# A two-pass RWKV-7/pooling trunk: the second pass projects r, key, value and low-rank columns for two blocks per product

## The chip, the cores and the metric

The kernel runs on one core of a Trainium2 chip. The metric is the device time of one execution in microseconds. The kernel before takes 2581.55 us (median of 3 runs, 2581.06 to 2581.68).

## What is computed

Sequence length 4096, width 1024, one layer. Cut to what matters here:

```python
u = rms_norm(h, norm_gain) * (1.0 + scale) + shift
proj = u @ w_in                      # 1024 -> 3200 columns
y_pool = multiscale_pool(proj[pool value]) * silu(proj[pool gate])
# RWKV branch: pf = proj columns r | k | v | w_down | a_down
pf = pf + (token_shift(pf) - pf) * mu           # token t needs token t-1
w_log = -softplus(-(w0 + tanh(wd) @ w_lora_up)) - 0.5;  decay = exp(-exp(w_log))
a = sigmoid(a0 + ad @ a_lora_up)
kk = normalized(k * k_k);  k = k * (1 + (a - 1) * k_a)
# per head, a 64x64 state S, in order of time:
#   S = S*decay + (S @ -kk) outer (kk*a) + v outer k;   y = S @ r
y_rwkv = group_norm(y) + bonus(r, k, v);  y_rwkv *= silu(proj[rwkv gate])
h = h + gate * (concat(y_pool, y_rwkv) @ w_out);  out = rms_norm(h, final_gain)
```

All arithmetic is float32.

## The kernel before

The kernel has two passes. The first (`first_pass`, 8 tiles of 512 tokens) does the norm, the pooling branch and its half of the output product, and stores two things in DRAM: the partial result (`h1`) and the normalized input, transposed, as `xt` (32 blocks of 128 tokens, for each block and partition 8 x 128 numbers in one piece). The second pass (`second_pass`) does the RWKV branch in 32 blocks of T2 = 128 tokens, each made of two chunks of 64.

The TensorE program of one block n is `front(n)`, then `back(n)`. `front` has the head variance of block n-1, the bonus sum (`rk_sum`, bank 1), transposes of v and of the key pair BK, and the Gram products of both chunks (line 1348). `back` has six inversion steps (lines 1238 and 1241), and then for both chunks: products with the state (line 1270, called R below), the solve (1281), the state product (1294) and the output products (1302, 1303). VectorE and ScalarE take each result out of PSUM and prepare the next operand. Between two inversion steps, VectorE masks and transposes (`factor`, lines 1774 and 1786), and ScalarE copies the step's result to LX (`take_step`, line 1493); step i+1 waits for both.

While all that happens, TensorE fills its time with the **projection of the next block**: 17 column tiles of 128 weights (13 of r, key, value and low-rank columns, 4 of the gate), each of 8 products over the 1024 inputs. They are cut in **slots** of 4 products, 34 per block, that `fill(k)` puts between the other work: 6 slots before step 0, 3 after each of steps 0 to 3, 2 after step 4, 1 after step 5, then 2, 2, 1 and 2 between the chunk's products, and the rest, 6, at the end of `back`. The first 20 slots of a block use 128 columns of weights per instruction (line 1183), the last 14 use `by_halves`, two products with 64 columns of weights each (line 1164). A float32 product is two MATMUL records in the trace.

The tiles come in five groups of PSUM banks 0 and 1 in turn (`GROUPS`, line 1105):

```python
GROUPS = [(12, 1, 0), (0, 4, 1), (4, 4, 0), (8, 4, 1), (13, 4, 0)]   # first tile, tiles, bank
```

When a group is complete (`group_ps`), ScalarE's `take_group` copies it, scaled by mu, one column to the right (line 1432, `prev`), and VectorE's `shift` (line 1675) adds the token-shift mixture into `mix`. Only then may the bank be used again. The column of the last token is carried to the next block by a copy on GpSimd (line 1617). ScalarE and VectorE run their instructions strictly in the written order: on ScalarE `take_group` 0 stands before `take_step(0)`, group 1 before `take_step(3)`, group 2 before the low-rank exponentials and `take_u(0)`, group 3 after `take_u(1)`, the gate group at the end. On VectorE, the way from the state sum of chunk 1 to the next block's step 0 is one long row of operations: the key (lines 1714, 1715), `shift` 3, BK (1722), the operands LA (1813, 1819), the state, the bonus (1825), masks of the Gram products (1830, 1835), WT and W (1791, 1786).

SyncE loads the transposed input of block n+2 (`load_xT`, line 1129) when the projection of block n is complete. The prologue (line 1384) projects block 0 in one go during the end of the first pass.

Of the kernel before, what the change touches and what calls it, by code (L numbers as in the profile page):

```python
# [126 lines left out]
def build(nc, A, out):  # L127
# [3 lines left out]
    with ctx:  # L131
# [42 lines left out]
        W2 = ((0, 4, 0), (4, 4, 4096), (8, 4, 8192), (13, 4, 12288), (12, 1, 16384))  # L174
# [786 lines left out]
        def second_pass():  # L961
# [10 lines left out]
            xT = [new(f"xT2{j}", [P, KT, T2]) for j in range(2)]  # L972
            mix = new("mix", [P, MIX, T2])
            prev = new("prev", [P, MIX, 1 + T2])
# [4 lines left out]
            egx = new("egx", [P, NP, T2])  # L979
# [3 lines left out]
            t2 = new("t2", [P, NP, T2])  # L983
            k2 = new("k2", [P, NP, T2])
            rk = new("rk", [P, NP, T2])
# [42 lines left out]
            group_ps = signal("group_ps", 5)  # L1028
            rg_ready = signal("rg_ready", 1)
            mix_in = signal("mix_in", MIX)  # L1030
            mix_ready = signal("mix_ready", 4)
            carry_ready = signal("carry_ready", 1)
# [10 lines left out]
            gprev_ready = signal("gprev_ready", 1)  # L1043
            exps_ready = signal("exps_ready", 3)
# [111 lines left out]
            def tensor(pe):  # L1156
# [10 lines left out]
                def project(m, n, par, prologue=False, halves=False):  # L1167

                    gr, q, k0 = SLOTS[m]
                    t0, w, b = GROUPS[gr]  # L1170
                    if q == 0 and k0 == 0:
                        if gr == 0:
                            pe.wait_ge(xT_loaded[par], (n - par) * 8 + 16)
                            if not prologue:
                                s.wait(bt_ready, 2)
                        elif gr > 1:
                            nx.wait(mix_ready, gr - 1)
                        elif not prologue:
                            s.wait(prep_ready, 1)
                        if prologue:  # L1180
                            pe.wait_ge(w2_in[[g[0] for g in W2].index(t0)], 32 if t0 == 12 else 16)
                    for k in range(k0, k0 + KT // 2):
                        last = (by_halves if halves else nc.tensor.matmul)(  # L1183
                            bank[b][:, q * P:(q + 1) * P], w2_tile(k, t0 + q), xT[par][:, k, :],
                            start=(k == 0), stop=(k == KT - 1))
                    if q == w - 1 and k0:
                        last.then_inc(group_ps.sem, 1)

                def low_rank():
                    nx.wait(mix_ready, 1)  # L1190
                    nx.wait(th_ready, 1)
                    for p in range(NP):
                        for i, (part, rhs) in enumerate(((slice(0, LORA), th[0:LORA, :]), (slice(LORA, P), mix[LORA:P, 12, :]))):
# [28 lines left out]
                def inverses(fill, other, first):  # L1222
# [31 lines left out]
                    fill(1, halves=True)  # L1254
# [51 lines left out]
                def front(n, first=False):  # L1306
# [16 lines left out]
                    for p in range(NP):  # L1323
                        for r, c in QUARTERS:
                            j = int(r == c)
                            last = nc.tensor.matmul(bank[(5, 7)[j]][half(c), p * HD:(p + 1) * HD], mix[half(r), 8 + p, j * C:(j + 1) * C],
# [25 lines left out]
                def back(n, first=False, ahead=True, par=0):  # L1352
# [6 lines left out]
                    def fill(k=1, halves=False):  # L1359
                        for _ in range(k):  # L1360
                            if ahead and m[0] < len(SLOTS):
                                project(m[0], n + 1, 1 - par, halves=halves)
# [6 lines left out]
                    if ahead:  # L1369
                        low_rank()  # L1370
                    solve(0)
                    fill(2, halves=True)
                    state_and_output(0, first)
                    fill(2, halves=True)
# [3 lines left out]
                    fill(1, halves=True)  # L1378
                    solve(1)
                    fill(2, halves=True)  # L1380
                    state_and_output(1)
                    fill(len(SLOTS), halves=True)

                def prologue():
                    nx.block(0)
                    pe.wait_ge(sum_ready1.sem, sum_ready1.at(N1 - 1, 7 * PT))
                    for m in range(len(SLOTS)):
                        project(m, 0, 0, prologue=True)
                    low_rank()
                    key_norm()  # L1390

                def blocks():
# [3 lines left out]
                    front(1)  # L1396
                    back(1, par=1)
                    front(2)
                    for n in range(2, N2 - 3, 2):
                        back(n)  # L1400
                        front(n + 1)
                        back(n + 1, par=1)
                        front(n + 2)
                    back(N2 - 2)
                    front(N2 - 1)
                    back(N2 - 1, ahead=False, par=1)
# [7 lines left out]
            def scalar(act):  # L1414
# [5 lines left out]
                def take_group(n, gr):  # L1420
# [3 lines left out]
                    t0, w, b = GROUPS[gr]  # L1424
                    nx.wait(group_ps, gr + 1)
                    if gr == 4:
# [8 lines left out]
                def exp_tanh():  # L1435
                    hd.wait(mix_ready, 1)
# [551 lines left out]
```

## Time and profile before

| | us |
|---|---|
| median of 3 runs | 2581.55 |
| the profiled execution | 2582.14 |
| its span, first to last instruction | 2580.4 |
| PE busy | 2489.7 (96%) |
| PEld (weight loads) busy | 2054.8 (80%) |
| DVE busy | 1657.4 (64%) |
| ACT busy | 1147.4 (44%) |
| POOL busy | 415.3 (16%) |
| mean granted TensorE clock | 0.984 |

The first pass and the prologue end at about 763 us, where the second pass's first inversion step starts; the regular blocks then take about 57 us each, and the last block ends the span. PE is the matrix product on TensorE, PEld its weight loads, DVE is VectorE, ACT ScalarE, POOL GpSimd. A busy PE is not a PE at its peak, since records of products overlap. What a product costs is therefore read from the distance of starts.

### The profile page before, as it was taken

Reading aid. Unit: us, or ns where it says so; the run is one execution under the profiler, and the core shown is the slowest. Engines: PE = TensorE matmul, PEld = TensorE weight load, DVE = VectorE, ACT = ScalarE, POOL = GpSimd, SP = SyncE. Lnnn points to the kernel's source line nnn. Section 1 sums busy time; section 2 is a strip of 40 time slices with the busy share of each in tenths; the row PEclk is TensorE's granted clock in tenths of the full one; section 3 lists DMA queues with packets and bytes.
Section 4 is the critical chain, followed back from the end, with each engine's and each line's share of the span. In section 5 each row is a group of like instructions: output and inputs, shape, how many; then the busy total and the mean of one; then the engine's idle time right before and its main releaser. Section 6 shows DMA issues by size and latency. Waiting matters only on the chain.

```text
span 2580.4 us, 73686 instructions
## 1 busy us (share of the span) xinstructions
PE 2489.7 (96%) x30485; PEld 2054.8 (80%) x30485; DVE 1657.4 (64%) x3459; ACT 1147.4 (44%) x2539; POOL 415.3 (16%) x565
## 2 busy tenths in 40 slices
PE   4999999999999999999999999999999999999995
PEld 4777666777768888888888888888888888888883
DVE  4563344334357777777777777767777777777774
ACT  4332223331124555454455554544555445455552
POOL 1410111110111111111111111211111112111110
PEclk7999999999999999999999999999999999999997
DMA  6613321334510010000001010000110000001000
GB/s 236 208 63 130 130 98 56 114 122 172 187 50 10 35 35 33 28 26 26 26 26 43 26 35 26 26 26 26 35 35 28 33 26 26 26 26 43 26 19 25
DMA packets 72618, 152.91 MB, mean 59 GB/s; under 512 B 3801, under 2 KB 38190, under 8 KB 71342
## 3 DMA queue, kind: packets, MB, share of 16 engines
q1 hardware_dynamic: 68878, 141.62, 15.6%
q10 hardware_dynamic: 3488, 7.34, 0.8%
q8 instruction: 231, 3.78, 0.6%
q14 instruction: 21, 0.17, 0.0%
HBM read 98.61 MB, written 50.33 MB: 58 GB/s over the span
## 4 chain that ended last, share of the span: by engine, by line
PE 85%; DVE 9%; issue 3%; ACT 1%; DMA 1%; SPq 0%; DVEq 0%; ACTq 0%
PE banks L1183 21%; PE banks L383 15%; PE banks L1164 14%; PE banks L1218 9%; PE banks L459 9%; PE banks L1238 7%; DVE SM L1830 2%; PE banks L1281 1%; PE banks L1294 1%; PE banks L1194 1%; PE banks L1348 1%; PE banks L1270 1%; DMA gc<-in_w_ada 1%; PE banks L1302 1%; PE banks L1303 1%
## 5 line engine op out<-in xcount | busy, mean ns | idle before, releaser
L1183 PE MATMUL banks<-xT,wts 128*128 128x128 f32 x5232 | 633.7, 279 | 0.0
L1183 PEld LDWEIGHTS banks<-xT,wts 128*128 128x128 f32 x5232 | 598.2, 192 | 30.9 <-issue 27.1
L1493 ACT ACTIVATE LX<-banks 128x512 f32<-128x512 f32 (+1 forms) x384 | 185.0, 524 | 643.4 <-DVE WT L1774 437.3
L1164 PE MATMUL banks<-xT,wts 128*64 128x128 f32 x6944 | 420.1, 274 | 0.0
L1164 PEld LDWEIGHTS banks<-xT,wts 128*64 128x64 f32 x6944 | 380.2, 137 | 6.3
L1610 POOL TENSOR_TENSOR BK<-k,egi 64x512 f32<-64x512 f32 x64 | 96.0, 1500 | 930.4 <-ACT egi L1462 889.4
L1218 PE MATMUL banks<-wo,Y 128*128 128x512 f32 x512 | 233.8, 600 | 4.7 <-DVE Y L1734 4.7
L383 PE MATMUL banks<-ts,wts 128*128 128x256 f32 x1024 | 233.3, 381 | 0.0
L1774 DVE TENSOR_TENSOR WT<-banks,level_mask 128x256 f32<-128x256 f32 x256 | 102.6, 422 | 194.8 <-PE banks L1238 186.8
L459 PE MATMUL banks<-wo,yc 128*128 128x512 f32 x512 | 224.1, 596 | 0.0
L383 PEld LDWEIGHTS banks<-ts,wts 128*128 128x128 f32 x1024 | 195.9, 191 | 27.5 <-DVE fgain L845 0.5
L459 PEld LDWEIGHTS banks<-wo,yc 128*128 128x128 f32 x512 | 97.0, 192 | 118.6 <-issue 118.5
L383 PE MATMUL banks<-xT,wts 128*128 128x256 f32 x768 | 180.2, 383 | 6.7 <-ACT xT L563 4.7
L1599 POOL TENSOR_TENSOR LA<-SM,ones 64x256 f32<-64x256 f32 x128 | 93.4, 730 | 529.0 <-DVE Y L1734 515.2
L1432 ACT ACTIVATE prev<-banks,vec 128x128 f32<-128x128 f32 x416 | 121.8, 374 | 120.4 <-PE banks L1183 114.0
L1218 PEld LDWEIGHTS banks<-wo,Y 128*128 128x128 f32 x512 | 93.7, 193 | 100.4 <-issue 94.8
L383 PEld LDWEIGHTS banks<-xT,wts 128*128 128x128 f32 x768 | 146.8, 192 | 30.4 <-ACT xT L563 5.4
L1238 PEld LDWEIGHTS banks<-LX,W 64*64 64x64 f32 x4096 | 111.9, 134 | 58.0 <-issue 50.3
L1238 PE MATMUL banks<-LX,W 64*64 64x128 f32 x4096 | 143.1, 278 | 2.5 <-ACT LX L1493 1.6
L1675 DVE SCALAR_TENSOR_TENSOR mix<-banks,omu,prev 128x128 f32<-128x128 f32 x416 | 119.3, 345 | 27.7 <-ACT prev L1432 10.3
L845 DVE TENSOR_TENSOR fgain<-banks,fgain 128x256 f32<-128x256 f32 x96 | 40.7, 424 | 138.0 <-PE banks L383 137.7
L1786 DVE STREAM_TRANSPOSE W<-WT 128x256 f32<-128x256 f32 x320 | 121.8, 419 | 0.0
(193 smaller groups left out, 3649.1 us busy)
## 6 DMA issues: line engine op xcount, KB each, us to landing
wo<-in_x SPq DMA_DIRECT2D x8, 2048.0 KB, 9.4
xt_dram<-xT SPq DMA_DIRECT2D x32, 512.0 KB, 8.6
xr<-in_x SPq DMA_DIRECT2D x32, 512.0 KB, 5.7
h_dram<-xr SPq DMA_DIRECT2D x32, 512.0 KB, 2.7
xT<-xt_dram SPq DMA_DIRECT2D x32, 512.0 KB, 3.3
gate_row<-h_dram SPq DMA_DIRECT2D x32, 512.0 KB, 3.4
out<-gate_row SPq DMA_DIRECT2D x32, 512.0 KB, 2.6
wts<-in_w_in SPq DMA_DIRECT2D x4, 2048.0 KB, 7.9
```

Of the source, the lines that this page charges most:

```text
L383: last = nc.tensor.matmul(product_ps(g, i), w1[:, g, left, k], right[:, k], start=(k == 0), stop=(k == KH - 1))
L459: last = nc.tensor.matmul(bank[BANK_OUT[h]][:, :], yc[:, k, j * P:(j + 1) * P], wo1[:, k, h * 512:(h + 1) * 512], start=(k == 0), stop=(k ...
L1164: last = nc.tensor.matmul(o[half(c)], lhsT[:, half(c)], rhs, start=start, stop=stop)
L1183: last = (by_halves if halves else nc.tensor.matmul)(bank[b][:, q * P:(q + 1) * P], w2_tile(k, t0 + q), xT[par][:, k, :], start=(k == 0), ...
L1218: last = nc.tensor.matmul(bank[(4, 7)[h]][:, :], Y[:, p], wo2[:, p, h * 512:(h + 1) * 512], start=(p == 0), stop=(p == NP - 1))
L1238: last = nc.tensor.matmul(step_banks[a][half(c), j, p * P:(p + 1) * P], W[h, a, j, p], (LX if i else AI)[h, a, j, p].rearrange(flat), star ...
L1432: nx(nc.scalar.activation(prev[:, t, 1:], src, ACT.Copy, scale=v("mu", t)), mix_in, hold=False)
L1493: s(nc.scalar.activation(to, of, ACT.Copy), lx_ready, hold=False)
L1610: hd(nc.gpsimd.tensor_tensor(BK[h, :, :, 1 - e], chunks(k2[h]), chunks(egi[h]), ALU.mult), kt_ready if e else head_pool)
L1675: ins = nc.vector.scalar_tensor_tensor(out=mix[:, t], in0=bank[b][:, q * P:(q + 1) * P], scalar=omu[:, t:t + 1], in1=prev[:, t, 0:T2], op0 ...
L1774: s(nc.vector.tensor_tensor(WT[:, a], left(a)[:, :, 0:2, 0], mask_of(level_mask[i]), ALU.mult), wt_ready, hold=False)
L1786: s(nc.vector.transpose(W[:, a].rearrange("p j q t -> p (j q t)"), WT[:, a].rearrange("p j q t -> p (j q t)")), w_ready, hold=False)
```

## The change

The 13 tiles of r, key, value and low-rank columns are no longer projected for one block at a time, but for two, with 256 columns of x per product. What was one list of groups is now two, in turn. While an even block's back runs, the next, odd, block is projected: tile 12 and tiles 4 to 9 for that block and the one after it. While an odd block's back runs, the next, even, block is projected: tiles 0 to 3, 10 and 11 for that block and the one after it. The gate's 4 tiles stay with one block. All products now have 128 columns of weights; `by_halves` is no longer used in the projection. A slot is 2 products of 256 columns, or 4 of the gate's: 36 slots in the first list, 32 in the second. The positions and numbers of `fill` are unchanged but for the rest at the end.

`mix` holds two blocks; `prev` only holds one group per bank; the last token's column is kept in `carry`, by small copies on ScalarE in `take_group`, and the copy on GpSimd is gone. `egx`, its subtraction on VectorE and its exponential on ScalarE are gone; `decay` has one more column per chunk, set to 1, instead. `xT` holds two blocks side by side for each of the 8 input tiles, so that a load now writes 8 pieces of 512 bytes per partition, where it wrote one of 4096. The order in which w_in's columns lie in `wts` is changed. The prologue projects the first list for block 0 alone and the second list for blocks 0 and 1.

```diff
-            GROUPS = [(12, 1, 0), (0, 4, 1), (4, 4, 0), (8, 4, 1), (13, 4, 0)]
-            MIXED = [1, 5, 9, 13]
-            SLOTS = [(gr, q, k) for gr, (_, n, _) in enumerate(GROUPS) for q in range(n) for k in (0, KT // 2)]
+            GROUPS = ([(0, 2, 0), (2, 2, 1), (10, 1, 0), (11, 1, 1), (13, 4, 0)],
+                      [(12, 1, 0), (4, 2, 1), (6, 2, 0), (8, 2, 1), (13, 4, 0)])
+            GATE = 4
+            SLOTS = [[(gr, q, k) for gr, (_, w, _) in enumerate(g) for q in range(w) for k in range(0, KT, KT // 2 if gr == GATE else KT // 4)]
+                     for g in GROUPS]
...
-                    sp.dma_start(xT[par][:, :, :], rows_of(xt, n)).then_inc(xT_loaded[par], 16)
+                    sp.dma_start(xT[:, :, par, :], rows_of(xt, n)).then_inc(xT_loaded[par], 16)
...
+                    for k in range(k0, k0 + (KT // 2 if gr == GATE else KT // 4)):
+                        if gr == GATE:
+                            to, x = bank[b][:, q * P:(q + 1) * P], xT[:, k, par]
+                        elif seg is None:
+                            to, x = bank[b][:, q * 2 * T2:(q + 1) * 2 * T2], xT[:, k].rearrange("p s t -> p (s t)")
+                        else:
+                            to, x = both(b, q, seg), xT[:, k, seg]
+                        last = one(to, w2_tile(k, t0 + q), x, start=(k == 0), stop=(k == KT - 1))
...
 # take_group, ScalarE
+                    nc.scalar.activation(before[:, 0:w, f, 0:1], col.unsqueeze(2), ACT.Copy)
                     for q in range(w):
-                        src = bank[b][:, q * P:(q + 1) * P]
-                        t = t0 + q
-                        nx(nc.scalar.activation(prev[:, t, 1:], src, ACT.Copy, scale=v("mu", t)), mix_in, hold=False)
+                        to, of = (before[:, q, :, 1:], both(b, q)) if seg is None else (before[:, q, seg, 1:], both(b, q, seg))
+                        ins = nc.scalar.activation(to, of, ACT.Copy, scale=v("mu", t0 + q))
+                    nx(ins, taken)
+                    if seg is None:
+                        nx(nc.scalar.activation(before[:, 0:w, 1 - f, 0:1], before[:, 0:w, f, T2:T2 + 1], ACT.Copy), mix_in, hold=False)
+                        f = 1 - f
+                    else:
+                        act.sem_inc(mix_in.sem, 1)
+                    nx(nc.scalar.activation(col.unsqueeze(2), before[:, 0:w, f, T2:T2 + 1], ACT.Copy), carried, hold=False)
...
-                    hd(nc.scalar.activation(egx[:, :, :], egx[:, :, :], ACT.Exp, scale=-DECAY), exps_ready)
...
 # vector
-                def decay_ahead():
-                    hd(nc.vector.tensor_tensor(egx[:, :, :], G[:, :, :], sig[:, 0], ALU.subtract), gprev_ready, hold=False)
...
 # gpsimd
-                    s.wait(mix_ready, 4)
-                    s(copy(prev[:, :, 0:1], prev[:, :, T2:T2 + 1], ones[:, 0:MIX].unsqueeze(2)), carry_ready)
```

Three places show how instructions move. The first is TensorE from the end of a block's back to step 1 of the next (`xT,wts` are projection products; 64x128 is a product by half of the weights; `AI,W` is step 0). Before, the same in every block:

```order
L1164 MATMUL banks<-xT,wts 64x128 x48
L1164 MATMUL banks<-rs,head_mean 64x512 x2
L1164 MATMUL banks<-rk,rk_sum 64x128 x8
L1326 MATMUL banks<-center,mix 64x64 x16
L1339 MATMUL banks<-ident,BK 128x64 x16
L1348 MATMUL banks<-LA,BK 128x128 x16
L1183 MATMUL banks<-xT,wts 128x128 x24
L1238 MATMUL banks<-AI,W 64x128 x16
L1183 MATMUL banks<-xT,wts 128x128 x12
```

Now, after an even block's back:

```order
L1207 MATMUL banks<-xT,wts 128x128 x32
L1171 MATMUL banks<-rs,head_mean 64x512 x2
L1171 MATMUL banks<-sig,rk_sum 64x128 x8
L1355 MATMUL banks<-center,mix 64x64 x16
L1368 MATMUL banks<-ident,BK 128x64 x16
L1377 MATMUL banks<-LA,BK 128x128 x16
L1207 MATMUL banks<-xT,wts 128x256 x12
L1267 MATMUL banks<-AI,W 64x128 x16
L1207 MATMUL banks<-xT,wts 128x256 x6
```

The rest before the variance is 32 products instead of 24 whole ones (48 halves); after an odd block's back it is 16. Behind the Gram products stand 12 wide products, where there were 24 narrow ones.

The second place is ScalarE between the copies BT of a front and the first LX of the inversion, for the loop's second (odd) block, whose next block is even. Before:

```order
L1521 ACTIVATE BT<-banks 128x512 x2
L1432 ACTIVATE prev<-banks,vec 128x128
L1493 ACTIVATE LX<-banks 128x512 x2
L1503 ACTIVATE UV<-Vt 64x256 x2
L1437 ACTIVATE th<-mix 64x128
L1493 ACTIVATE LX<-banks 128x512 x2
```

Now, in the odd block:

```order
L1569 ACTIVATE BT<-banks 128x512 x2
L88 ISA x2
L1472 ACTIVATE prev<-carry 128x2
L1475 ACTIVATE prev<-banks,vec 128x2x128 x2
L84 REGISTER_ALU
L1478 ACTIVATE prev<-prev 128x2
L1482 ACTIVATE carry<-prev 128x2
L88 ISA
L1541 ACTIVATE LX<-banks 128x512
```

(ISA and REGISTER_ALU rows are waits.) Ahead of the first LX copy, in place of one copy of one tile, stand the group of tiles 0 and 1: a small copy, two wide ones, a wait for them, and two small copies. In an even block it is one wide copy between the small ones.

The third place is SyncE, the load of the transposed input. Before:

```order
L1129 DMA xT<-xt_dram 128x1024
```

Now:

```order
L1136 DMA xT<-xt_dram 128x8x128
```

The number of bytes is the same, the pieces are eight times as many.

## Rows read from the trace of the kernel before

**Rows 1.** The page: the chain that ended last, by engine.

```profile
PE 85%; DVE 9%; issue 3%; ACT 1%; DMA 1%; SPq 0%; DVEq 0%; ACTq 0%
```

**Rows 2.** Busy time by stretch, columns as the heading row says: regular blocks, and end.

```profile
core 0: us, PE busy (x) PEld busy (x) DVE busy (x) ACT busy (x) POOL busy (x), PEclk, DMA share, GB/s
...
880.00:2500.00 1620.00, 1608.49 (x24768) 1379.72 (x24768) 1193.78 (x2634) 835.23 (x1968) 254.92 (x309) 1.00 0.08 29
2500.00:2580.40 80.40, 52.64 (x711) 37.29 (x707) 41.28 (x93) 27.77 (x58) 9.57 (x11) 0.79 0.08 28
```

**Rows 3.** Timeline of PE in one block: start us, length us, engine, line, operation.

```profile
1499.89 1.10 PE L1238 MATMUL banks<-LX,W 64*64 64x128 f32 x32
...
1527.36 0.69 PE L1294 MATMUL banks<-UV,BT 128*64 128x64 f32 x16
...
1536.68 5.46 PE L1164 MATMUL banks<-xT,wts 128*64 128x128 f32 x96
1541.92 1.08 PE L1164 MATMUL banks<-rs,head_mean 128*64 128x512 f32 x4
...
1545.16 2.04 PE L1348 MATMUL banks<-LA,BK 64*128 64x128 f32 x32
1547.13 5.62 PE L1183 MATMUL banks<-xT,wts 128*128 128x128 f32 x48
1553.10 1.10 PE L1238 MATMUL banks<-AI,W 64*64 64x128 f32 x32 [0.35 <-DVE W L1786]
1554.14 2.94 PE L1183 MATMUL banks<-xT,wts 128*128 128x128 f32 x24
1557.01 1.10 PE L1238 MATMUL banks<-LX,W 64*64 64x128 f32 x32
```

**Rows 4.** The chain that ended last, prologue: start us, length us, what.

```profile
684.50 30.37 PE banks L1183 x272
```

**Rows 5.** Timeline of PE in the first pass: products of 256 columns.

```profile
530.94 5.34 PE L383 MATMUL banks<-ts,wts 128*128 128x256 f32 x24
536.12 1.89 PE L383 MATMUL banks<-xT,wts 128*128 128x256 f32 x8
```

**Rows 6.** Timeline of DVE from the last state sum to W.

```profile
1536.03 0.88 DVE L1761 TENSOR_TENSOR stmp<-banks,SV 64x256 f32<-64x256 f32 x2 [0.23 <-PE banks L1294]
...
1539.44 1.13 DVE L1675 SCALAR_TENSOR_TENSOR mix<-banks,omu,prev 128x128 f32<-128x128 f32 x4
1540.70 1.42 DVE L1722 TENSOR_TENSOR BK<-t,egi 64x512 f32<-64x512 f32 x2
...
1546.02 0.69 DVE L1825 TENSOR_TENSOR bonus<-banks,mix 128x512 f32<-128x512 f32 x1
1546.85 1.50 DVE L1830 TENSOR_TENSOR SM<-banks,gram_mask 128x512 f32<-128x512 f32 x2
```

**Rows 7.** Waits in regular blocks: who, for whom, total us, times, longest us.

```profile
PE banks L1238 <- DVE W L1786: 4.7, 13, 0.4
```

**Rows 8.** Timeline of ACT: an LX pair, and the stretch up to u.

```profile
1498.84 1.08 ACT L1493 ACTIVATE LX<-banks 128x512 f32<-128x512 f32 x2 [6.08 <-DVE WT L1774]
...
1522.04 0.66 ACT L1493 ACTIVATE LX<-banks 128x256 f32<-128x256 f32 x2 [1.05 <-PE banks L1241]
...
1524.09 0.20 ACT L1479 ACTIVATE hstat<-hstat 128x1 f32<-128x1 f32 x1
1524.40 1.14 ACT L1432 ACTIVATE prev<-banks,vec 128x128 f32<-128x128 f32 x4
1525.42 1.16 ACT L1442 ACTIVATE sig<-banks,negv 128x128 f32<-128x128 f32 x4
...
1526.83 0.38 ACT L1498 ACTIVATE UV<-banks 64x256 f32<-64x256 f32 x1
```

**Rows 9.** Timeline of SP: the load of the transposed input.

```profile
1542.40 0.33 SPq L1129 DMA_DIRECT2D xT<-xt_dram  x1
```

**Rows 10.** DMA issues of the page: KB each, median us to landing.

```profile
xt_dram<-xT SPq DMA_DIRECT2D x32, 512.0 KB, 8.6
...
xT<-xt_dram SPq DMA_DIRECT2D x32, 512.0 KB, 3.3
```

**Rows 11.** Landing of the stores of xT (512-byte pieces), four queued at a time.

```profile
DMA to landing us min/median/max: 5.2/8.6/11.2
```

More of the change, by code:

```diff
@@ L978, in second_pass @@
             G = new("G", [P, NP, T2])
-            egx = new("egx", [P, NP, T2])
+            decay = new("decay", [P, NP, NC, 1 + C])
             egi = new("egi", [P, NP, T2])
@@ L1177, in project @@
                             nx.wait(mix_ready, gr - 1)
-                        elif not prologue:
+                        elif prologue:
+                            if seg is None:
+                                nx.wait(mix_ready, 4, back=1)
+                        else:
                             s.wait(prep_ready, 1)
                         if prologue:
[L1181 to L1185, printed above, removed]
@@ new lines, in project, with last_slot, w2_landed, low_rank @@
+                    if q == w - 1 and last_slot(par, m):
+                        last.then_inc(group_ps.sem, 1)
+                def last_slot(par, m):
+                    return m + 1 == len(SLOTS[par]) or SLOTS[par][m + 1][0] != SLOTS[par][m][0]
+                def w2_landed(t):
+                    i = next(i for i, g in enumerate(W2) if g[0] <= t < g[0] + g[1])
+                    return w2_in[i], 32 if W2[i][0] == 12 else 16
+                def low_rank(pb):
+                    nx.wait(mix_ready, 1, back=1 - pb)
@@ L1351, in front, with back @@
                                     last.then_inc(gram_ps.sem, 1)
-                def back(n, first=False, ahead=True, par=0):
+                def back(n, first=False, ahead=2, par=0):
                     s.block(n)
@@ new lines, in take_group @@
+                    f = par if seg is None else seg
+                    nx.count[taken] = nx.count[carried] = nx.count[mix_in] = gr
+                    if not (isinstance(n, int) and n < 1):
+                        nx.wait(carried, gr + 1, back=2)
+                    else:
+                        act.wait_ge(zero_ready, 1)
+                    nc.scalar.activation(before[:, 0:w, f, 0:1], col.unsqueeze(2), ACT.Copy)
+                    for q in range(w):
+                        to, of = (before[:, q, :, 1:], both(b, q)) if seg is None else (before[:, q, seg, 1:], both(b, q, seg))
+                        ins = nc.scalar.activation(to, of, ACT.Copy, scale=v("mu", t0 + q))
@@ L1523, in run @@
                     if ahead:
-                        s.wait(carry_ready, 1)
-                        take_group(n + 1, 0)
+                        seg = 1 if ahead == 1 else None
+                        take_group(n + 1, 1 - par, 0, seg)
                     if first:
@@ L1576, in scalar @@
                 hd.block(0)
-                take_group(0, 0)
-                exp_tanh()
-                for gr in range(1, 5):
-                    take_group(0, gr)
+                take_group(-1, 1, 0, 0)
+                exp_tanh(0)
+                for gr in range(1, GATE):
+                    take_group(-1, 1, gr, 0)
+                for gr in range(GATE + 1):
+                    take_group(0, 0, gr)
                 exp_low_rank(0)
@@ L1846, in run @@
                     if ahead:
-                        shift(n + 1, 0)
+                        shift(n + 1, 1 - par, 0, 1 if ahead == 1 else None)
                     factor(1)
@@ L1857, in run @@
                     if ahead:
-                        shift(n + 1, 1)
+                        shift(n + 1, 1 - par, 1, 1 if ahead == 1 else None)
                     last_factor()
@@ L1903, in prologue @@
                     dve.sem_inc(wo2_ready, 1)
-                    shift(0, 2)
-                    key()
-                    shift(0, 3)
+                    shift(-1, 1, 2, 0)
+                    key(0)
+                    shift(-1, 1, 3, 0)
+                    for i in range(GATE):
+                        shift(0, 0, i)
                     clamp(0)
```

185 lines of the change are left out of this document (101 added, 84 removed).

## The prediction

> **What bounds the kernel now.** I read the chain that ended last first: the reader sees 85% of it on PE and 9% on DVE [rows 1]. Then the busy times of the regular blocks: PE 1608 of 1620 us at full clock, and the clock falls only in the last 80 us, where nothing is left to project [rows 2]. So time is what PE does, unless it is made to wait. The timeline shows how near that is: step 0 at 1553.10 began after 0.35 us of waiting for DVE's W [rows 3], a wait that comes 13 times in the 28 regular blocks, 4.7 us in all, 0.17 per block [rows 7]. DVE works almost without a gap from the last state sum (1536.03) to W [rows 6]. ScalarE has two tight places: its second LX copy ended at 1499.92, when step 1 had just begun (1499.89) [rows 8, 3], and its copy of u ended at 1527.21, 0.15 before the product that reads it [rows 8, 3]. PE is the bound with two neighbours close behind, so an edit that shortens PE's work has to be followed on all three engines.
>
> **What a product costs.** From distances of starts; two records are one float32 product. Narrow, whole weights: 30.37 / 272 = 0.1117 us a record, 0.2234 a product [rows 4]. Narrow, by halves: (1541.92 - 1536.68) / 96 = 0.0546, four records, 0.2183 [rows 3]. Wide: (536.12 - 530.94) / 24 = 0.2158, 0.4317, which is 0.2158 per block served [rows 5]. So the wide product beats the whole narrow one by 3.4% and the halves by 1.1% only. A slot was 0.894 (whole) or 0.873 (halves); now a wide slot is 0.863 and a gate slot 0.894. A change of pattern costs some 0.2 more: 24 records took 2.87 until the next step began, not 2.68 [rows 3]. Nothing in the trace shows this for wide products, which could cost anything from 0 to the same; I take the same, since the row is of the same neighbours.
>
> The Trainium skill (Perfetto Trace Analysis, Identifying the Most-Contended Engine) judges TensorE by the busy share of weight loads, and that is 85% here [rows 2]; by it, halving the loads of 13 of 17 tiles should free much. Rows 5 speak against it: with loads half as frequent, a wide record takes just twice a narrow one less 0.008 us.
>
> **The sum over PE alone.** Before, per block: 80 whole products and 56 by halves, 17.87 + 12.23 = 30.10 us. Now, per pair of blocks: 104 wide and 64 gate products, 44.90 + 14.30 = 59.20, or 29.60 per block. That would be 0.5 per block, 1.0 per pair. But it is not evenly spread. Between step 0 and R of chunk 0 stand 15 slots in either kind: 15 x 0.863 instead of 14 x 0.894 + 0.873, **-0.44**. From there to the next step 0 stood 13 half and 6 whole slots, 16.71. After an even block's back it is now 7 + 6 wide and 8 gate, 11.22 + 7.15 = 18.37, **+1.66**; after an odd one 3 + 6 wide and 8 gate, 14.92, **-1.79**.
>
> **Even block.** -0.44 + 1.66. The rest before the variance is 64 records x 0.1117 = 7.15 instead of 5.24, so bonus and Gram products come 1.9 later, while DVE is ready earlier; PE keeps the bound and its old wait of 0.17 goes. ScalarE ahead of u: `take_group` 2 took 1.02 from start to the next group's start for four tiles [rows 8]. Now it is a small copy, two wide ones, a wait for their end, two small ones. A wide one has a pitch of 0.28 and a length of 0.38 (the pair of 128x256 copies) [rows 8], a small one a length of 0.20 (hstat) [rows 8] and a shorter pitch, I take 0.15 (bounds: 0.05 to 0.2): 0.15 + 0.28 + 0.38 + 0.06 + 0.15 + 0.2 = 1.2 to 1.3. U comes 0.25 later, and PE, which had 0.15 to spare and arrives 0.1 earlier, waits some 0.2. Sum: -0.44 + 1.66 - 0.17 + 0.2 = **+1.25**.
>
> **Odd block, step 1.** The next block's first group is now tiles 0 and 1, 8 slots, and only 6 stand before step 0. It is complete after step 0 (1.04), the change of pattern (0.2) and 8 more records (1.73) plus the end of the last (0.17): 3.15 after the start of step 0. ScalarE takes the group before LX of step 0: about 1.15 for the same sequence, then 0.6 for the first LX (half of the pair is 0.5, its length 0.6; the pair took 1.08 [rows 8]). So step 1 starts at 3.2 + 1.15 + 0.6 + 0.05 = 5.0, where PE is ready at 1.04 + 2.79 = 3.83. That is **a new wait of 1.15**. Late next is DVE, whose `shift` 0 then needs two wide instructions, but step 2 is 2.8 of PE work away and ScalarE and DVE have both done theirs. Before, the group (one tile) was complete far ahead of step 0.
>
> **Odd block, up to the next step 0.** PE could gain 1.79, but DVE's row bounds it. What falls out of it after 1536.03: `shift` 3 was four instructions, 1539.44 to 1540.70 with their wait; now one wide one of about 0.42 and the wait, so 0.75 less [rows 6]. Its other savings (the egx subtraction, 0.69, and `shift` 2) lie before 1536.03, where it waits for PE's state product anyway. Gram products, which waited for nothing, now wait for LA. I take **-0.75**, and PE idles 1.0 before step 0. Bounds: 0 (another wait in the same row) to -1.79. Sum of the odd block: -0.44 + 1.15 - 0.75 = **-0.05**.
>
> **Load.** The SP queue issues it at 1542.40, and the projection that used to need it much later needs it now in the next six slots, at 1547.13 [rows 9, 3]: 4.7 us. It took 3.3 in 4096-byte pieces [rows 10]. In pieces of 512 bytes the nearest rows are the stores of xT, which never landed under 5.2, but with four queued and other traffic [rows 11]. Between 3.3 and 5.2 I take 4, hidden; at 5.2 it costs 0.5 per block, 15 us. The skill (DMA: Bandwidth & Descriptors, Specifications) gives 512 bytes as the least size at line rate; by that the load stays hidden.
>
> **Ends.** The prologue's 136 narrow products took 30.37 and were on the chain [rows 4]. Now 56 + 32 narrow and 48 wide ones: 19.66 + 20.72 = 40.4, **+10.0**; ScalarE and DVE follow within a group's time. The counterpart is the back of block 30, which projects its 7 tiles at 128 columns: 15 slots of 0.447 instead of 0.89 save 6.6 in its first part, of which DVE's row between the steps gives back about 1.5, and its rest is 1 longer. I take **-4**; less if the clock falls earlier.
>
> **Total.** 15 pairs x (1.25 - 0.05) = +18, +10 - 4: **+24 us** on the profiled 2582.1, which was 0.6 over the median: 2606 as a median. About 0.2% (5 us) is what a measurement of this kernel can tell from no change.
>
> **Rivals.** *(A) PE's sum decides, faster.* If ScalarE and DVE cost nothing new, each pair gives 1.03, the old wait too, and perhaps half of the pattern changes (some eight per block at 0.1): -16 + 10 - 4 = -10, down to -30. For it speaks that PE is the bound; against it the two orders of ScalarE and DVE. It needs the wait at step 1 under 0.1, so group 0 taken before LX is due. 2573, chance 0.14. *(B) Weight loads bind*, as the skill's rule above has it: a wide product then costs as a narrow one, 52 x 0.2234 + 32 x 0.2234 = 18.8 us per block instead of 30.1, some 350 us in all, 2230. Rows 5 contradict it; 0.01. *(C) The load comes late or ScalarE's small copies cost their full length* (0.2, with waits): +12 to +30 on top, 2620 to 2635; nothing in the trace excludes it. 0.15. *(D) The terms cancel*: DVE's row yields the whole 1.79 and the step-1 wait is half, about -1.6 per pair, 2582; 0.10. *(E) The change does not do what it says* (products still narrow in the records): excluded by the instruction order. The forecast, 2592 to 2618, has 0.60.
>
> **Numbers.** Faster by over 0.2% is A and B, 0.15; within it D, 0.10; slower the forecast and C, 0.75. The range 2576 to 2626 leaves out most of A, B and the upper half of C, under 2 in 10.
>
> **What would show it.** Wide records 0.216 apart; PE waiting about 1.1 at step 1 of odd blocks for LX, and about 1 at their next step 0 for W; no wait there in even blocks, whose period is 1.2 longer; the prologue's projection near 40 us. It is wrong if step 1 does not wait, if PE waits for a DMA ahead of the six slots, or if odd and even periods do not differ in this sense.

## The result and the profile after

The changed kernel takes 2639.34 us (median of 4 runs, 2638.70 to 2643.38), the kernel before 2581.35 (4 runs): ratio 1.0228, 95% interval 1.0210 to 1.0246. It is **slower by 58 us**, 2.3%, where 24 were forecast and 2626 was the upper end of the range.

| | before | after |
|---|---|---|
| profiled execution, us | 2582.14 | 2638.91 |
| span | 2580.4 | 2637.2 |
| PE busy | 2489.7 | 2520.8 |
| PEld busy | 2054.8 | 1941.8 |
| DVE busy | 1657.4 | 1605.4 |
| ACT busy | 1147.4 | 1151.8 |
| mean granted clock | 0.984 | 0.984 |

The chain that ended last has the same shape as [rows 1], and the mean clock is the same, so the time is in PE's row: PE is busy 31 us longer although it issues a fifth fewer records, and it waits more. The chain by engine, and the two largest waits of PE between 830 and 2400 us (columns as in [rows 7]):

```profile
PE 84%; DVE 10%; issue 3%; ACT 2%; DMA 1%; SPq 0%; DVEq 0%; POOL 0%; ACTq 0%; POOLq 0%
```

```profile
PE banks L1267 <- ACT LX L1541: 14.3, 13, 1.1
PE banks L1267 <- DVE W L1834: 7.8, 13, 0.6
```

Starts of step 0 tell where it goes. Before, they lie 56.83 us apart after an even block's start and 57.12 after an odd one's, 113.95 for a pair (the wait for W of [rows 3, 7] came behind odd blocks alone, 0.35 at each, where the prediction spread it as 0.17 over all). Now it is **59.33 (even) and 57.61 (odd)**, 116.94 for a pair, +2.99. The whole span, by these starts:

| stretch | before | after | difference |
|---|---|---|---|
| up to step 0 of block 0 | 762.97 | 778.20 | +15.2 |
| block 0 | 49.57 | 52.30 | +2.7 |
| blocks 1 to 28, 14 pairs | 1595.1 | 1637.1 | +42.0 |
| the rest | 172.8 | 169.6 | -3.2 |

The timeline of PE, after (columns as in [rows 3]; first the way from an even block's last state product to step 1 of the odd block, then the same from the odd block to the even one; output products between 1323 and 1207 left out):

```profile
1512.51 0.69 PE L1323 MATMUL banks<-UV,BT 128*64 128x64 f32 x16
...
1514.10 7.41 PE L1207 MATMUL banks<-xT,wts 128*128 128x128 f32 x64
1521.44 1.08 PE L1171 MATMUL banks<-rs,head_mean 128*64 128x512 f32 x4
...
1524.70 2.03 PE L1377 MATMUL banks<-LA,BK 64*128 64x128 f32 x32
1526.66 5.45 PE L1207 MATMUL banks<-xT,wts 128*128 128x256 f32 x24
1532.10 1.10 PE L1267 MATMUL banks<-AI,W 64*64 64x128 f32 x32
1533.13 2.86 PE L1207 MATMUL banks<-xT,wts 128*128 128x256 f32 x12
1537.09 1.16 PE L1267 MATMUL banks<-LX,W 64*64 64x128 f32 x32 [1.10 <-ACT LX L1541]
...
1560.12 0.69 PE L1299 MATMUL banks<-SV,LA 128*64 128x64 f32 x16
...
1571.08 2.05 PE L1207 MATMUL banks<-xT,wts 128*128 128x128 f32 x16
1573.06 0.69 PE L1323 MATMUL banks<-UV,BT 128*64 128x64 f32 x16
...
1574.66 3.84 PE L1207 MATMUL banks<-xT,wts 128*128 128x128 f32 x32
...
1583.64 5.45 PE L1207 MATMUL banks<-xT,wts 128*128 128x256 f32 x24
1589.71 1.10 PE L1267 MATMUL banks<-AI,W 64*64 64x128 f32 x32 [0.62 <-DVE W L1834]
```

Three forecasts are there: step 1 of the odd block starts 4.99 after step 0 (forecast 5.0), with a wait of 1.10; step 0 of the even block waits for W, if 0.62 and not 1.0; step 0 of the odd block waits for nothing. ScalarE's row says why step 1 waits (timeline of ACT, after):

```profile
1535.25 0.21 ACT L1472 ACTIVATE prev<-carry 128x2 f32<-128x2 f32 x1 [9.04 <-PE banks L1207]
1535.36 0.82 ACT L1475 ACTIVATE prev<-banks,vec 128x256 f32<-128x256 f32 x2
1536.21 0.21 ACT L1478 ACTIVATE prev<-prev 128x2 f32<-128x2 f32 x1
1536.32 0.19 ACT L1482 ACTIVATE carry<-prev 128x2 f32<-128x2 f32 x1
1536.42 1.06 ACT L1541 ACTIVATE LX<-banks 128x512 f32<-128x512 f32 x2
```

It was idle for 9 us for the group's last record, 3.15 after step 0's start, took the group in 1.17, and only then copied LX; before, the LX pair had ended as step 1 began [rows 8].

What no term of the forecast held is between R of chunk 0 and the rest. From the start of R (1560.12) to the rest (1574.66) are 14.54 us; before it was 13.62 (1523.06 to 1536.68), **0.92 more**, in even and odd blocks alike, though by the distance of their records the 7 slots there take 6.0 us in even blocks and 6.2 in odd ones, where they took 6.1. One stretch of before, of 32 records, and its follower:

```profile
1528.77 1.97 PE L1164 MATMUL banks<-xT,wts 128*64 128x128 f32 x32
1530.52 1.07 PE L1164 MATMUL banks<-rn,head_sum 128*64 128x512 f32 x4
```

32 records in 1.75 us are 0.0547 each, the same distance as in the long stretch [rows 3]: by halves, this stretch of projection costs its records and nothing else. In the kernel after, the 16 records at 1571.08 take 1.98 until the state product, where 16 x 0.1117 = 1.79, and the output products ahead of 1574.66 take 1.60, where they took 1.40.

### The profile page after: what moved, and what is told of

Same layout as the page of the kernel before. It is cut to its first block, busy times and chain, and to the rows that moved or that the text cites. A ratio compares the mean times of both kernels' runs of the same rounds, so it can differ in the third digit from the quotient of the medians.

```text
span 2637.2 us, 60141 instructions
## 1 busy us (share of the span) xinstructions
PE 2520.8 (96%) x23797; PEld 1941.8 (74%) x23797; DVE 1605.4 (61%) x3226; ACT 1151.8 (44%) x2694; POOL 391.9 (15%) x534
## 4 chain that ended last, share of the span: by engine, by line
PE 84%; DVE 10%; issue 3%; ACT 2%; DMA 1%; SPq 0%; DVEq 0%; POOL 0%; ACTq 0%; POOLq 0%
PE banks L1207 33%; PE banks L383 14%; PE banks L1247 8%; PE banks L459 8%; PE banks L1267 6%; PE banks L1171 2%; DVE SM L1877 2%; PE banks L1323 2%; PE banks L1310 1%; PE banks L1223 1%; PE banks L1299 1%; PE banks L1377 1%; PE banks L1331 1%; DMA ts<-in_w_ada 1%; PE banks L1332 1%
## 5 line engine op out<-in xcount | busy, mean ns | idle before, releaser
L1207 PE MATMUL banks<-xT,wts 128*128 128x256 f32 (+1 forms) x5488 | 1050.6, 344 | 6.5 <-issue 3.8
L1207 PEld LDWEIGHTS banks<-xT,wts 128*128 128x128 f32 x5488 | 850.4, 191 | 119.4 <-issue 32.4
L1660 POOL TENSOR_TENSOR BK<-k,egi 64x512 f32<-64x512 f32 x64 | 82.4, 1287 | 953.8 <-ACT egi L1512 899.5
L1472 ACT ACTIVATE prev<-carry 128x2 f32<-128x2 f32 (+1 forms) x132 | 27.1, 205 | 374.1 <-PE banks L1207 339.7
L383 PEld LDWEIGHTS banks<-xT,wts 128*128 128x128 f32 x768 | 147.1, 192 | 28.9 <-ACT xT L563 5.4
L1726 DVE SCALAR_TENSOR_TENSOR mix<-banks,omu,prev 128x256 f32<-128x256 f32 (+1 forms) x215 | 94.5, 472 | 44.9 <-ACT prev L1478 28.1
L1850 DVE STREAM_TRANSPOSE WL<-banks 32x128 f32<-32x128 f32 x128 | 39.8, 311 | 123.1 <-PE banks L1267 120.0
L1877 DVE TENSOR_TENSOR SM<-banks,gram_mask 128x512 f32<-128x512 f32 x128 | 88.5, 692 | 37.5 <-PE banks L1377 27.5
```

The costliest lines, as they stand in the source:

```text
L383: last = nc.tensor.matmul(product_ps(g, i), w1[:, g, left, k], right[:, k], start=(k == 0), stop=(k == KH - 1))
L1207: last = one(to, w2_tile(k, t0 + q), x, start=(k == 0), stop=(k == KT - 1))
L1660: hd(nc.gpsimd.tensor_tensor(BK[h, :, :, 1 - e], chunks(k2[h]), chunks(egi[h]), ALU.mult), kt_ready if e else head_pool)
L1726: ins = nc.vector.scalar_tensor_tensor(out=mix[:, t, of], in0=both(b, q)[:, of], scalar=omu[:, t:t + 1], in1=prev[:, b, q, of, 0:T2], op0= ...
L1877: s(nc.vector.tensor_tensor(SM[j][e].rearrange("p a b c -> p a (b c)"), bank[((2, 3), (4, 7))[j][e]][:, :].rearrange("p (a b) -> p a b", b=P),
```

## Experiments

The first question was what the 0.92 is. Theory 1 (shape): next to products with 64 columns of weights, short stretches with 128 columns pay at each entry and exit; why they should is a guess of the expectations below, which no run tests. Theory 2 (ScalarE): the longer `take_group` delays u and the solve. Runs are set against the kernel before on the same chip (2579.8 there; 2579.1 for the last).

**b_whole.** The kernel before, all projection with whole weights.

```diff
-                        last = (by_halves if halves else nc.tensor.matmul)(
+                        last = nc.tensor.matmul(
```

> The kernel before with 128 columns of weights in every projection product (the last 14 slots of a block no longer by halves). Theory 1 (shape): the short stretches of projection between the chunk's products lose time when they have 128 columns of weights, since a whole load does not hide beside the 64-column loads around it: the stretch from the start of R of chunk 0 to the rest was 13.62 us before and 14.54 in the changed kernel, 0.92 more. Then this kernel is slower than before by 0.9 a block in those stretches, and by 24 products at 0.223 instead of 0.218 plus one change of pattern, 0.3, in the rest: 31 x 1.2 = +37 us, 2618. Theory 2 (ScalarE): the 0.92 comes from the longer take_group, which this kernel has not: then it only costs 56 x 0.005 = 0.3 a block, +9 us, 2590.

Measured: 2618.22 us, ratio 1.0148 (1.0131 to 1.0165): +38 us where theory 1 said +37 and theory 2 +9. Step 0 is 58.19 apart in every block, 1.22 more than before's mean of 56.98: 1.01 more from R to the rest, 0.31 in the rest and 0.16 between step 0 and R, less 0.27 ahead of step 0, where PE no longer waits for W. The stretch that answers to the one above, and its surroundings (timeline of PE, b_whole):

```profile
1542.96 0.69 PE L1294 MATMUL banks<-UV,BT 128*64 128x64 f32 x16
...
1544.55 2.05 PE L1183 MATMUL banks<-xT,wts 128*128 128x128 f32 x16
1546.54 1.08 PE L1164 MATMUL banks<-rn,head_sum 128*64 128x512 f32 x4
```

The same 8 products now take 1.99, not 1.75, and the output products ahead of them take longer too: 1.59 from the state product to the projection, where it was 1.41. Of the 1.22, 0.29 is the distance of the records (56 products at 0.2234 instead of 0.2183); the rest comes with the changes of shape. Nothing of the wide groups, of `take_group` or of the load is in this kernel, so the shape of the weights alone is enough for this loss. Theory 2 is not needed for it.

**a_halves_late.** The changed kernel, all slots after step 5 by halves (the fills not shown, up to the rest, are changed in the same way).

```diff
-                    one = nc.tensor.matmul
+                    one = by_halves if halves else nc.tensor.matmul
...
-                    fill(1)
+                    fill(1, halves=True)
...
-                    fill(2)
+                    fill(2, halves=True)
...
```

> The changed kernel, the slots after step 5 by halves (64 columns of weights), wide and gate ones, as they were before. Theory 1 (shape): the 0.92 us a block of the short stretches comes back, and some 0.3 in the rest: 31 x 1.1 = 34 us, 2605; the odd blocks give less if VectorE's row up to W binds them (PE already idles 0.6 there): then 15 x 1.2 = 18 us, 2621. Theory 2 (ScalarE's take_group): no change beyond 0.1 a block, 2636.

Measured: 2614.22 us, ratio 1.0137 (1.0120 to 1.0154), 25 less than the changed kernel. Even blocks go from 59.33 to 58.09, **-1.24**, odd ones from 57.61 to 57.02, **-0.59**. In even blocks 0.15 of it lies between step 0 and R, 0.73 from R to the rest (14.53 to 13.80) and 0.35 in the rest. Theory 1, with its reservation for odd blocks: there PE now waits for VectorE twice (timeline of PE, a_halves_late):

```profile
1569.36 2.06 PE L1377 MATMUL banks<-LA,BK 64*128 64x128 f32 x32 [0.68 <-DVE LA L1866]
1571.35 5.45 PE L1207 MATMUL banks<-xT,wts 128*128 128x256 f32 x24
1577.42 1.10 PE L1267 MATMUL banks<-AI,W 64*64 64x128 f32 x32 [0.63 <-DVE W L1834]
```

Theory 2 is not wholly void: in even blocks R to the rest is still 0.18 longer than before, because PE now waits 0.3 for u, which ScalarE copies behind its longer `take_group` (the wait is in the list under c_balance).

**a_step1.** The changed kernel; in odd blocks ScalarE takes the first group behind the first LX pair.

```diff
-                    if ahead:
-                        seg = 1 if ahead == 1 else None
+                    seg = 1 if ahead == 1 else None
+                    if ahead and par == 0:
                         take_group(n + 1, 1 - par, 0, seg)
...
                     take_step(0)
+                    if ahead and par:
+                        take_group(n + 1, 1 - par, 0, seg)
```

> The changed kernel, with ScalarE taking the next block's first group behind the first LX pair instead of ahead of it, in odd blocks alone. Both theories: PE's wait at step 1 of odd blocks (1.10 us in the trace) goes. If nothing takes its place, 15 x 1.1 = 16.5 us less, 2623. If the wait only covered another one (shift 0 on VectorE now late for step 2), less than half of it, 2632 or more.

Measured: 2623.11 us, ratio 1.0169 (1.0152 to 1.0186), 16 less. Odd blocks go from 57.61 to 56.38, even ones stay at 59.33 (59.32). The wait was real and covered no other.

**b_halves_all.** The kernel before, every slot of the blocks by halves.

```diff
-                        last = (by_halves if halves else nc.tensor.matmul)(
+                        last = (nc.tensor.matmul if prologue else by_halves)(
```

> The kernel before with all slots of the blocks by halves (the prologue as it was). Theory 1 (shape): the fills between inversion steps, whose neighbours have 64 columns of weights too, lose their 0.2 us of change of pattern each, and products cost 0.218 instead of 0.223: a fill of 12 products goes from 2.87 to 2.62. Five fills and one of 24 products: 4 x 0.25 + 0.2 + 0.3 = up to 1.5 us a block less for PE, of which VectorE's row before step 0 holds back 0.3 or more: 31 x 1.0 = -31 us, 2550. Theory 2, in which only ScalarE matters: within 5 us of 2581.

Measured: 2576.58 us (10 runs), ratio 0.9987 (0.9977 to 0.9996): 3 us less, not 31. Two things failed in the expectation. A fill between steps took 2.77 to the next step, not 2.62: beside the 64x64 products of a step, halves pay 0.15 where whole weights paid 0.2. And the output half behind such a fill takes 3.63 instead of 3.53. What the 6 slots ahead of step 0 gain is lost to W (timeline of PE, b_halves_all; after the line shown, the next block waited 0.24):

```profile
1544.10 5.46 PE L1164 MATMUL banks<-xT,wts 128*64 128x128 f32 x96
1550.10 1.10 PE L1238 MATMUL banks<-AI,W 64*64 64x128 f32 x32 [0.54 <-DVE W L1786]
```

So the gain of halves is a matter of their neighbours, and ahead of step 0 the kernel before already stood at VectorE's row.

**a_narrow.** The changed kernel, each wide slot as 4 products of 128 columns.

```diff
-                    for k in range(k0, k0 + (KT // 2 if gr == GATE else KT // 4)):
+                    z, hk = divmod(k0 // 2, 2)
+                    two = gr != GATE and seg is None
+                    for k in range(4 * hk, 4 * hk + 4) if two else range(k0, k0 + (KT // 2 if gr == GATE else KT // 4)):
...
+                        elif two:
+                            to, x = both(b, q, z), xT[:, k, z]
```

> The changed kernel, each wide slot issued as 4 products of 128 columns (one half of a tile's 1024 inputs for one of the two blocks) instead of 2 of 256; order, groups, ScalarE and VectorE as in the change. It shows what the 256 columns bring by themselves. By the distances of starts a slot goes from 0.863 to 0.894: 28 slots in even blocks, +0.87; in odd blocks 24, of which the 9 before the next step 0 lie beside VectorE's row, +0.46: 15 x 1.33 + 1 in the prologue = +21, 2660. If wide products brought more than that (fewer changes and loads), 2680 or more; if nothing, 2639.

Measured: 2658.49 us, ratio 1.0306 (1.0288 to 1.0323): 19 more than the change, where 21 were expected. Even blocks are 60.00 apart (+0.67), odd ones 58.11 (+0.50). So 256 columns per product bring what the distances of records say, some 19 us, and no more.

**c_joint.** The two edits that helped together: a_halves_late and a_step1 (the diffs above).

> The changed kernel with both edits together: the slots after step 5 by halves, and in odd blocks the first group taken behind the first LX pair. If the two losses are separate they add: 2639 - 25 - 16 = 2598, pairs of blocks of 58.1 + 55.8 = 113.9, the same as the kernel before, and what stays above it is the prologue's 15. If one hides the other: 2605 or more.

Measured: 2596.40 us, ratio 1.0063 (1.0046 to 1.0080); 58.08 and 55.79, 113.87 a pair against 113.95 before. The losses add. Nothing is left of the 2.99 in the regular blocks, and the total is still 17 us above before: 15 of it was the prologue's loss in the change.

**c_pro.** c_joint, and two edits of the prologue.

```diff
                 swap_residual(N1 - 1)
+                early_load()
                 store(N1 - 1)
...
-                    if ahead == 2:
+                    if ahead == 2 and not first:
                         load_xT(n + 2, par)
...
+                def early_load():
+                    load_xT(2, 0)
...
                     shift(-1, 1, 1, 0)
+                    shift(-1, 1, 2, 0)
+                    key(0)
+                    shift(-1, 1, 3, 0)
                     dve.wait_ge(w2_in[4], 32)
                     for t in range(NP):
...
-                    shift(-1, 1, 2, 0)
-                    key(0)
-                    shift(-1, 1, 3, 0)
                     for i in range(GATE):
```

> c_joint, and in the prologue: the load of block 2's input is issued ahead of the last stores of the first pass (PE waited 3.67 us for it before step 0 of block 0), and the products of w_out and the gate on VectorE come behind the mixtures of block 0 (PE waited 0.75 behind them). 4.4 us less than c_joint: 2594. If the wait for the load only covered VectorE's row ahead of step 0 (W was ready 3.1 us after the Gram products began plus 5), 1 to 2 us less.

Measured: 2590.95 us, ratio 1.0044 (1.0027 to 1.0060), 5.4 less than c_joint in the medians. In the profiled executions step 0 of block 0 starts at 773.94; it was at 778.20 in the change and at 780.62 in c_joint. A part of that is the first pass, which no edit touches: the prologue's projection starts at 683.02 in the change, 685.68 in c_joint and 682.68 here. From that start to step 0 are 95.2, 94.9 and 91.3 us, so the two edits brought 3.7 to 3.9. The wait for the load had cost more than its 3.67, as the part on the prologue below shows, and the wait for W has taken the place of a part (timeline of PE, c_pro):

```profile
766.35 5.45 PE L1211 MATMUL banks<-xT,wts 128*128 128x256 f32 x24
773.94 1.10 PE L1271 MATMUL banks<-AI,W 64*64 64x128 f32 x32 [2.15 <-DVE W L1840]
```

The medians of c_joint and c_pro are 5 us apart, with runs 4 to 5 us wide each, so the size in the median is only roughly known.

**c_balance.** c_pro, with one slot moved out of the inversion of odd blocks into their rest, and one of even blocks ahead of step 0, to where PE waited for VectorE.

```diff
-                        fill(3 if i < LV else 2)
+                        fill((2 if par and i == LV - 1 else 3) if i < LV else 2)
...
-                    fill(6)
+                    fill(6 if par else 7)
```

> c_pro, and two slots moved into stretches in which PE waits for VectorE's row after odd blocks (0.68 ahead of the Gram products, 0.63 ahead of step 0): in odd blocks one slot fewer after step 3, so one more in the rest; in even blocks 7 slots instead of 6 ahead of step 0. PE's work is the same. If those waits are what is left of the imbalance, up to 1.3 a pair, 15 x 1.1 = 16 us less than c_pro, 2578; if another wait takes their place (the bonus or Gram products late for VectorE), under 8.

Measured: 2568.82 us, ratio 0.9958 (0.9941 to 0.9974), 22 less than c_pro. Pairs are 57.21 + 55.09 = 112.30, **1.57 less than c_joint's, 1.65 less than before's**. Expected was 1.1 to 1.3, the two waits for VectorE. Both are gone. First the largest waits of PE between 830 and 2400 us in c_joint, then in c_balance:

```profile
PE banks L1377 <- DVE LA L1868: 9.4, 14, 0.7
PE banks L1267 <- DVE W L1836: 9.0, 14, 0.7
PE banks L1323 <- ACT UV L1546: 4.2, 14, 0.3
```

```profile
PE banks L1327 <- ACT UV L1550: 4.3, 14, 0.3
PE banks L1211 <- issue: 1.3, 1, 1.3
```

The two waits were 18.4 us over the 14 pairs, 1.3 a pair; by distances of starts they cost more, 1.58: from the variance products to the Gram products are 3.25 us where they were 4.13 (0.88), and the 7 slots ahead of step 0 take 6.24 where 6 took 6.08 with the wait (0.70 of the 0.86 of a slot). The wait for u is as it was.

This is the first version of the changed kernel below the kernel before, by 11 us or 0.4%, and it is below b_halves_all as well, by 8 us.

**c_pre_halves.** c_balance, the slots ahead of step 0 by halves too.

```diff
-                    fill(6 if par else 7)
+                    fill(6 if par else 7, halves=True)
```

> c_balance, the 6 or 7 wide slots ahead of step 0 by halves too. Theory 1 (shape): that stretch is entered from Gram products with 128 columns of weights and left to 64-column ones; in the changed kernel its 24 records took 5.44 us from start to start of step 0, 5.18 of it by their distance. By halves up to 0.2 a block less, 31 x 0.2 = 6 us, 2563, if VectorE's row does not bind (PE had no wait for W left in c_balance, DVE's margin is unknown). If the loss is in the neighbours' loads and not in the slots, no change, 2569.

Measured (5 runs): 2566.82 us, ratio 0.9950 (0.9937 to 0.9964). Not to be told from c_balance; blocks are 57.22 and 55.05 apart. The stretch takes the same time by halves (timeline of PE, c_pre_halves), 5.45 from start to step 0:

```profile
1604.32 5.40 PE L1175 MATMUL banks<-xT,wts 128*64 128x256 f32 x48
1609.77 1.10 PE L1271 MATMUL banks<-AI,W 64*64 64x128 f32 x32
```

So the 0.26 over its records is not a matter of the slots' shape there. It stands between products with 64 rows (Gram) and 64x64 ones; the fills between steps stand between 64x64 ones; the stretch where halves were free stands between products with 128 rows and 64 columns.

## Why the prediction was right in kind and wrong in size

**What a product costs: right.** The prologue of the changed kernel has 96 wide and 64 narrow records in one stretch: 27.9 us by the forecast's distances, 28.10 in the trace up to the end of the last. And a_narrow confirms the value of 256 columns, 19 us, by its own measurement. The rival that weight loads bind (B) is out: PEld's busy time fell by 113 us and the kernel got slower.

**The step that failed: the change of pattern.** The prediction took 0.2 for each change, from a stretch of whole weights beside inversion steps, and "the same" for wide products. It thereby let the stretches by halves pay it as well, so that it dropped out of the difference. The term it lacked is some 0.8 to 0.9 a block for the four short stretches between R and the rest, 0.2 for the rest itself and 0.15 for the slot after step 5: b_whole measures their sum at 1.22 a block with the distance of records in it, a_halves_late gives back 1.24 in even blocks and 0.59 in odd ones, where VectorE binds: 1.8 a pair, 25 us over the 14 pairs. It could have been suspected from the trace before: 32 records in 1.75 us, to the next operation, show no change cost. The rows of one kind of stretch had been used for all.

**Even block.** Forecast +1.25, measured +2.50. By stretches: step 0 to R -0.28 (forecast -0.44), R to the rest +0.92 (+0.13, with the wait for u), the rest +2.10 (+1.91), from there to step 0 -0.22 (-0.36). Most of the miss is the step above.

**The wait for u: misread.** The prediction took the 0.15 between the end of u's copy and the product that reads it for time to spare. In none of the runs does that product start less than 0.14 after the copy, so 0.15 is the handover and PE was waiting for u already: from the solve to the state product are 2.64 us in chunk 0 before, and 2.41 in chunk 1 with the same products between. In even blocks of the change it is 2.66, so the forecast 0.2 came to next to nothing while the shape's loss filled the time; with halves (a_halves_late) it is 2.87, and the 0.2 is there.

**Odd block, step 1: right**, 1.10 for 1.15, and a_step1 shows it is worth 1.23 a block, 16 us.

**Odd block up to step 0: right in mechanism.** The wait for W is there (0.62, forecast 1.0); the projection's loss of shape filled a part of PE's idle time, so that the shape cost 0.6 in odd blocks and 1.2 in even ones. VectorE's row, from its first operation on the state sum to W's product, became 1.23 shorter (17.07 to 15.84), not 0.75: `shift` 3 gave 0.74, as forecast, and the two products of the key 0.47, which no term held (last section). Odd blocks together: forecast -0.05, measured +0.49.

**Load: right.** The median time to landing is 4.1 us (forecast 4), and no regular block waits for it. DMA issues of the page, after:

```profile
xT<-xt_dram SPq DMA_DIRECT2D x32, 512.0 KB, 4.1
```

**Prologue: the work right, the waits missed.** Forecast +10.0, measured +15.2; from the projection's start to step 0 it is 16.6 (95.2 for 78.6), since the first pass ended 1.3 earlier in this execution. The projection itself is some 10 us longer. Besides, PE waits for VectorE's mixtures twice in it, after 24 and after 56 products, each time to use bank 0 again (1.94 and 0.75), and before the 6 slots of block 0 it waits 3.67 us for the load of block 2. That is the sign "if PE waits for a DMA ahead of the six slots", though in one block alone. The prediction placed that load by a regular block. In block 0 it is issued behind the last stores of the first pass (timelines of PE and of SP, after):

```profile
690.48 7.41 PE L1207 MATMUL banks<-xT,wts 128*128 128x128 f32 x64 [1.94 <-DVE mix L1726]
698.65 28.10 PE L1207 MATMUL banks<-xT,wts 128*128 128x256 f32 x160 [0.75 <-DVE mix L1726]
...
771.23 7.04 PE L1207 MATMUL banks<-xT,wts 128*128 128x256 f32 x24 [3.67 <-issue]
```

```profile
742.75 20.86 SPq L301 DMA_DIRECT2D h_dram<-xr  x4
766.98 0.56 SPq L1136 DMA_DIRECT2D xT<-xt_dram  x1
```

The wait had a sequel: behind it the 24 records took 6.97 us to step 0, where they take 5.44 in other blocks, because the granted clock had fallen to 0.50, its lower level of 1.2 GHz (busy time by stretch, after, columns as in [rows 2]). In c_pro, without the wait, it stays at 1.00 there and the 24 records take 5.45.

```profile
772.00:774.00 2.00, 2.00 (x6) 1.55 (x6) 1.97 (x3) 0.00 (x0) 1.84 (x3) 0.50 0.00 0
```

So the late load cost 3.67 and 1.53, 5.2 us; against it stands the wait of 1.98 for W that the kernel before had there.

**The tail** gave 3.2, forecast 4, but half of it by luck. The back of block 30, the only source of the forecast, gave 1.9 (57.31 to 55.42). The last block, in which nothing is projected, was 1.8 shorter at a granted clock of 0.72 in its first 18 us where it was 0.67, and 0.81 where it was 0.74 in the 20 after them; nothing in the forecast holds that.

**The sum**: 15.2 + 2.7 + 42.0 - 3.2 = 56.8 but for rounding, the whole difference of the spans. Taken back one by one, the shape of the weights is 25 us of it and the wait at step 1 is 16; the prologue is 15. The sign did not hang on the step that failed: a_halves_late, with the shape's loss taken out, is still 34 us slower than the kernel before, where 24 were forecast. Rival C (2620 to 2635) came nearest in number, but not by its reasons: ScalarE took the group in 1.17, as forecast (1.15), and the load is late in block 0 only.

## What to carry to other kernels

A matrix product's price has two parts, the distance of its records in a long stretch and what it costs to come in and go out between neighbours of another shape; with short stretches the second can exceed all that a wider operand gains, so read it at every kind of place that the edit touches, for the old form as well as for the new. When work is paired over two iterations, look at each iteration by itself: here the same work had up to 1.7 us more in one and waits in the other, and moving two slots was worth more (22 us) than the wide products (19 us). And follow first-iteration loads by their own queue, not by the steady state.

## What was not expected of the hardware

- Projection by halves (64 columns of weights) had no cost of entry or exit between products with 128 rows and 64 columns (32 records in 1.75 us), but 0.15 between 64x64 ones, and 0.26 between Gram products and step 0 (wide, by halves), as much as whole weights. Whole weights cost about 0.2 a stretch, in part in the products ahead of it: 0.2 in a fill between steps (2.87 for 2.68), and 0.22 in the mean of the four stretches between R and the rest (b_whole: 1.01, less 0.14 for the distance of 28 products). Why this is so was not tried.
- VectorE's product of key and rate (128x512, line 1715 before, 1763 after) took 1.65 us in nearly all blocks before and 0.69 in nearly all after, while the product ahead of it (line 1714 before, 1762 after) went from 0.69 to 1.2. GpSimd computes its half of BK beside them: before, from 1535.72 for 3.05 us, over both products (starts 1536.94 and 1537.67); after, from 1572.79 for 2.62 us, over most of the first one (1574.78) and none of the second (1575.99). So the slow product always had GpSimd beside it, but before the first one had it too and took 0.69; whether GpSimd is the cause is not shown. VectorE's row gained 0.4 us a block by it, which no term of the prediction held. DVE's two instructions by name:

```profile
L1715 DVE SCALAR_TENSOR_TENSOR t<-kk,sig x32: 691/1652/1661, 731.3 to 2506.0; 128x512 f32<-128x512 f32 x32
```

```profile
L1763 DVE SCALAR_TENSOR_TENSOR rn<-kk,sig x32: 691/692/1644, 743.4 to 2563.4; 128x512 f32<-128x512 f32 x32
```
